# 32 tokens' experts by gathered rows, beside dense U and V for the other 224

## The reference

```python
q = (ht @ w_q).reshape(T, PEER_HEADS, 2, PEER_HALF)
scores = jnp.einsum('thcd,hckd->thck', q, sub_keys)
# top 16 of each half, top 16 of their sums -> idx, g = softmax(top_s)
act = jax.nn.gelu(jnp.einsum('pd,phkd->phk', hb, u[ib]))
out = jnp.einsum('phk,phkd->pd', gb * act, v[ib])
```

## Time and profile before

| | |
|---|---|
| device time, three runs | 2462.65 us median (2459.61 to 2463.94) |
| the profiled execution | span 2461.2 us from first to last instruction; its device time is not recorded apart |
| busy | PE 2372.8, DVE 1667.5, ACT 1447.1, POOL 498.6 us |
| granted TensorE clock | 0.992 over the span |
| DMA | 449.67 MB, 183 GB/s mean |

### The profile page before, as it was taken

How to read it: one execution, slowest core, us unless ns; L and a number is a source line. 1 busy time by engine, 2 the same in 40 slices (tenths; PEclk the granted TensorE clock), 3 DMA queues, 4 the chain that set the end, 5 groups by cost and what they waited for, 6 DMA issues and landing times.

```text
span 2461.2 us, 50127 instructions
## 1 busy us (share of the span) xinstructions
PE 2372.8 (96%) x16310; PEld 2175.1 (88%) x16314; DVE 1667.5 (68%) x3882; ACT 1447.1 (59%) x3296; POOL 498.6 (20%) x417
## 2 busy tenths in 40 slices
PE   8998989999999999999999989899999999999998
PEld 8997888999999878888899978889999998788887
DVE  5667775577876676666656667755778767666666
ACT  5576755555655655555555676555555556555555
POOL 0000200007767400000000003000177773000000
PEclk9999999999999999999999999999999999999999
DMA  5554465456666446566544535654566664466664
GB/s 207 191 186 142 167 246 177 152 180 187 172 188 172 137 145 222 216 210 220 198 148 171 175 134 203 213 179 154 179 184 176 187 182 109 171 221 213 219 216 162
DMA packets 165203, 449.67 MB, mean 183 GB/s; under 512 B 48060, under 2 KB 58228, under 8 KB 164852
## 3 DMA queue, kind: packets, MB, share of 16 engines
...
HBM read 429.44 MB, written 21.66 MB: 183 GB/s over the span
## 4 chain that ended last, share of the span: by engine, by line
PE 87%; ACT 5%; DVE 5%; issue 2%; DMA 2%; ACTq 0%; POOL 0%; DVEq 0%; POOLq 0%; SPq 0%
PE bank L301 16%; PE bank L303 16%; PE bank L302 16%; PE bank L316 10%; PE bank L318 10%; PE bank L317 10%; PE bank L1613 2%; DVE w_lo L283 2%; ACT w_hi L270 2%; DMA raw<-stream 1%; ACT L343 1%; PE bank L393 1%; PE bank L1073 1%; PE bank L1595 1%; PE bank L1046 1%
## 5 line engine op out<-in xcount | busy, mean ns | idle before, releaser
L283 DVE TENSOR_TENSOR w_lo<-raw,w_hi 128x512 fp32r<-128x512 f32 x1512 | 1027.6, 690 | 718.2 <-ACT w_hi L270 704.6
L270 ACT ACTIVATE w_hi<-raw 128x512 fp32r<-128x512 f32 x1512 | 904.5, 626 | 384.7 <-PE bank L318 313.0
L301 PE MATMUL bank<-h_hi,w_hi 128*128 128x256 f32 x3360 | 963.6, 287 | 14.1 <-DVE w_lo L283 13.9
L302 PE MATMUL bank<-h_lo,w_hi 128*128 128x256 f32 x3360 | 952.5, 283 | 0.0
L303 PE MATMUL bank<-h_hi,w_lo 128*128 128x256 f32 x3360 | 952.4, 283 | 0.0
L301 PEld LDWEIGHTS bank<-h_hi,w_hi 128*128 128x128 f32 x3360 | 646.2, 192 | 25.9 <-DVE w_lo L283 18.8
L302 PEld LDWEIGHTS bank<-h_lo,w_hi 128*128 128x128 f32 x3360 | 646.8, 193 | 0.5
L303 PEld LDWEIGHTS bank<-h_hi,w_lo 128*128 128x128 f32 x3360 | 646.5, 192 | 0.0
L1204 POOL DMA_INDIRECT spread_w<-mass,cell_at x256 | 429.1, 1676 | 444.7 <-DVE mass L1491 298.0
L316 PE MATMUL bank<-w_hi,a_hi 128*128 128x512 f32 x1088 | 426.9, 392 | 10.6 <-DVE a_lo L411 5.6
L317 PE MATMUL bank<-w_lo,a_hi 128*128 128x512 f32 x1088 | 426.0, 392 | 0.0
...
## 6 DMA issues: line engine op xcount, KB each, us to landing
...
spread_w<-zeros POOLq DMA_DIRECT2D x32, 512.0 KB, 15.2
h_hi<-spread_w POOLq DMA_DIRECT2D x32, 512.0 KB, 4.8
...
spread_w<-mass,cell_at POOLq DMA_INDIRECT x256
...
```

The costliest lines, as they stand in the source:

```text
L270: act.activation(w_hi[:, (ring % 2) * 2 + k, :], raw[:, slot, sub, 512 * k:512 * k + 512], ACT.Copy).then_inc(w_hi_done, 1)
L283: dve.tensor_tensor(w_lo[:, q, :], raw[:, slot, sub, 512 * k:512 * k + 512], w_hi[:, q, :].bitcast(F32), ALU.subtract).then_inc(w_parts, 1)
L301: pe.matmul(ps, hi, rhs_hi(4 * k + c), start=first, stop=False)
L302: pe.matmul(ps, hi, rhs_lo(4 * k + c), start=False, stop=False)
```

## The change

32 tokens of the first tile (its lanes 96 to 127) leave the dense path. h, `A` and the U matmuls keep 224 columns: first the second tile, then 96 tokens of the first. For the 32 tokens, ScalarE's queue copies their pick numbers (`own_at`) and weights (`mass`) to `lane`, where 128 lanes are 4 groups of 32 tokens with 32 picks each. 64 indirect gathers per layer on GpSimd's queue bring one row of 4 KB per lane into a ring of four (`row`): 32 of U, 32 of V. VectorE forms the 32 dots with `h_rep`, ScalarE their gelu, VectorE sums the weighted V rows in `own`. Two matmuls fold the four groups and VectorE adds the result to x. `h_rep` comes from two matmuls after the scores and a gain row loaded by SP. Rows 0 to 3 are fetched inside the scatters of head 6, rows 4 to 7 behind the last scatter, rows 8 to 63 between the fetches of `spread_w`. Dots 0 to 7 stand at eight of the last U blocks, dots 8 to 31 at every second V block from 0, the sums at every second V block from 48. Scatters and spread products cover 96 lanes. `spread_w` is 96 wide and is zeroed in pieces of 128 floats, six per partition, in place of two of 512. In V the first tile's stationary has 96 columns, the moving side stays 512.

```diff
+N_OWN = 32
+N_DENSE = SEQ - N_OWN
+N_FIRST = P - N_OWN
+LANE_GROUPS = P // N_OWN
+OWN_PICKS = P // LANE_GROUPS
+RING = 4
+EARLY_DOTS = 8
...
-        spread_w = [nc.dram_tensor(f"spread_w{l}", (P, KEYS, P), F32, kind="Internal").ap() for l in range(DEPTH)]
+        spread_w = [nc.dram_tensor(f"spread_w{l}", (P, KEYS, N_FIRST), F32, kind="Internal").ap() for l in range(DEPTH)]
...
+        MIX_COLS = (slice(0, P), slice(P, 2 * P))
+        PEER_COLS = (slice(P, P + N_FIRST), slice(0, P))
...
-                    pool.dma_start(spread_w[layer][8 * i:8 * i + 8].rearrange("e (a b) t -> (e a) (b t)", a=16).rearrange("p (n f) -> p n f", f=512),
-                                   spread(zeros[:].rearrange("p (n f) -> p n f", n=1), 1, 2)).then_inc(cleared.sem, 16)
+                    pool.dma_start(spread_w[layer][8 * i:8 * i + 8].rearrange("e (a b) t -> (e a) (b t)", a=16).rearrange("p (n f) -> p n f", f=128),
+                                   spread(zeros[:].rearrange("p (n f) -> p n f", n=1), 1, 6)).then_inc(cleared.sem, 16)
...
-            A = sb(part, "A", [P, KEYS, SEQ])
+            A = sb(part, "A", [P, KEYS, N_DENSE])
+            row = sb(part, "row", [P, RING, D])
+            h_rep = sb(part, "h_rep", [P, D])
+            lane = sb(part, "lane", [P, 2, OWN_PICKS])
+            lane_at = sb(part, "lane_at", [P, 2, OWN_PICKS], U32)
+            dots = sb(part, "dots", [P, OWN_PICKS])
...
+            DOT_AT = (-12, -11, -10, -9, -3, -2, -1, 0)
...
-            spread_tile = [h_hi[:, 4 * i:4 * i + 4, :].rearrange("p c s -> p (c s)").bitcast(F32).rearrange("p (k t) -> p k t", t=P) for i in range(2)]
+            spread_tile = [h_hi[:, 4 * i:4 * i + 3, :].rearrange("p c s -> p (c s)").bitcast(F32).rearrange("p (k t) -> p k t", t=N_FIRST) for i in range(2)]
...
+                def fetch_row(n):
+                    i, values = n % RING, n // OWN_PICKS
+                    if n >= RING:
+                        pool.wait_ge(row_used.sem, row_used.base + n - RING + 1)
+                    pool.indirect_dma_start(row[:, i, :], None, stream_rows if values else u_rows,
+                                            bass.IndirectOffsetOnAxis(ap=lane_at[:, values, n % OWN_PICKS:n % OWN_PICKS + 1], axis=0)).then_inc(row_in[i].sem, 16)
                 pool.wait_ge(cleared.sem, cleared.base)
...
-                        pool.indirect_dma_start(cells, bass.IndirectOffsetOnAxis(ap=cell_at[:, h, r:r + 1], axis=0), mass[:, h, r:r + 1], None,
+                        pool.indirect_dma_start(cells, bass.IndirectOffsetOnAxis(ap=cell_at[0:N_FIRST, h, r:r + 1], axis=0), mass[0:N_FIRST, h, r:r + 1], None,
                                                 compute_op=ALU.add).then_inc(scattered.sem, 16)
+                        if (h, r) == (6, 12):
+                            pool.wait_ge(lanes_done.sem, lanes_done.base + 1)
+                            pool.wait_ge(rep_done.sem, rep_done.base + 1)
+                            for n in range(RING):
+                                fetch_row(n)
+                for n in range(RING, 2 * RING):
+                    fetch_row(n)
                 pool.wait_ge(scattered.sem, scattered.base + 16 * P)
                 pool.wait_ge(up_read.sem, up_read.base + 2 + B_V)
                     pool.dma_start(spread_tile[i % 2], spread_w[layer][:, 8 * i:8 * i + 8, :]).then_inc(spread_in[i % 2].sem, 16)
                 fetch(0)
                 fetch(1)
-                for i in range(2, 16):
-                    pool.wait_ge(spread_done.sem, spread_done.base + i - 1)
-                    fetch(i)
+                for n in range(2 * RING, 2 * OWN_PICKS):
+                    if n % 4 == 0 and n // 4 < 16:
+                        i = n // 4
+                        pool.wait_ge(spread_done.sem, spread_done.base + i - 1)
+                        fetch(i)
+                    fetch_row(n)
...
+                sp.dma_start(row[:, 0, :], spread(ffn_g[layer:layer + 1], 0, P)).then_inc(gain_row_in.sem, 16)
...
+                        if r == 2 and k == at + 6:
+                            act.wait_ge(own_kept.sem, own_kept.base + 2)
+                            act.wait_ge(mass_done.sem, mass_done.base + 2)
+                            for g in range(LANE_GROUPS):
+                                for i, kept in enumerate((own_at, mass)):
+                                    act.dma_start(lane[N_OWN * g:N_OWN * g + N_OWN, i, :].rearrange("p (h k) -> p h k", h=PEER_HEADS), kept[N_FIRST:P, :, 4 * g:4 * g + 4]).then_inc(lanes_in.sem, 16)
...
+                eights(0, 6)
+                act.wait_ge(row_used.sem, row_used.base + OWN_PICKS)
+                act.activation(dots[:], dots[:], ACT.Gelu_apprx_tanh).then_inc(own_gelu.sem, 1)
+                eights(6, 15)
...
+                def repeat_own():
+                    dve.wait_ge(rep_mm.sem, rep_mm.base + 1)
+                    dve.wait_ge(gain_row_in.sem, gain_row_in.base + 16)
+                    for k in range(2):
+                        cols = slice(512 * k, 512 * k + 512)
+                        ins = dve.tensor_tensor(h_rep[:, cols], row[:, 0, cols], bank[4 + k][:, :], ALU.mult)
+                    ins.then_inc(rep_done.sem, 1)
+                def lane_rows():
+                    dve.wait_ge(lanes_in.sem, lanes_in.base + 2 * LANE_GROUPS * 16)
+                    code = lane[:, 0, :]
+                    num, key = whole[:, 0:OWN_PICKS], dots[:]
+                    ch(dve.tensor_copy(num, code))
+                    dve.tensor_scalar(lane_at[:, 0, :], code, float(layer * KEYS * KEYS), None, ALU.add)
+                    ch(dve.tensor_scalar(num, num, 7, None, ALU.logical_shift_right))
+                    ch(dve.tensor_copy(key, num))
+                    ch(dve.tensor_scalar(code, code, float(KEYS), float(first_row_v(layer)), ALU.mult, ALU.add))
+                    dve.scalar_tensor_tensor(out=lane_at[:, 1, :], in0=key, scalar=float(1 - KEYS * KEYS), in1=code, op0=ALU.mult, op1=ALU.add).then_inc(lanes_done.sem, 1)
                 def masses(r):
...
+                        dve.tensor_copy(own_at[N_FIRST:P, mine, :], sel_i[N_FIRST:P, 0:ROUND_HEADS[r], :]).then_inc(own_kept.sem, 1)
+                        dve.tensor_scalar(cell_at[:, mine, :], sel_i[:, 0:ROUND_HEADS[r], :], float(N_FIRST), consts[:, C_ROW:C_ROW + 1], ALU.mult, ALU.add)
                         half(2)
...
+                def row_dot(i, wait, to):
+                    dve.wait_ge(row_in[i].sem, wait)
+                    dve.scalar_tensor_tensor(out=row[:, i, :], in0=row[:, i, :], scalar=1.0, in1=h_rep[:], op0=ALU.mult, op1=ALU.mult, accum_out=to).then_inc(row_used.sem, 1)
...
+                    n = DOT_AT.index(b - B_V) if b - B_V in DOT_AT else None
+                    if n is not None:
+                        row_dot(n % RING, row_in[n % RING].base + 16 * (n // RING + 1), dots[:, n:n + 1])
...
+                spread_product(0, 0, 0, 0)
+                part_lo(dve, src, 0, 0, N_DENSE)
+                dve.memset(own, 0.0)
+                ch(dve.tensor_scalar(turn_own, iota, consts[:, C_LANE:C_LANE + 1], None, ALU.is_equal))
+                def sixteen(n, first, i):
+                    if i in (3, 11):
+                        spread_product(1 - i // 8, n, first, 1 + i // 8)
+                    k = 16 * first + i
+                    split_lo(dve, n * 16 + (B_V + k + 1), (i + 1) % 4)
+                    part_lo(dve, src, n * 16 + (k + 1), (i + 1) % 2, N_DENSE)
+                with dve.Fori(0, 3) as n:
                     for i in range(16):
-                        if i in (3, 11):
-                            spread_product(1 - i // 8, n, 1 + i // 8)
-                        ahead_v(n * 16 + i, n * 16 + (B_V + i), i % 4, n, i)
+                        sixteen(n, 0, i)
+                        if i % 2 == 0:
+                            j = EARLY_DOTS + i // 2
+                            row_dot(j % RING, n * 32 + (row_in[j % RING].base + 16 * (j // RING + 1)), dots[:, bass.ds(n * 8 + j, 1)])
+                dve.wait_ge(own_gelu.sem, own_gelu.base + 1)
+                ch(dve.tensor_tensor(dots[:], dots[:], lane[:, 1, :], ALU.mult))
+                with dve.Fori(0, 4) as n:
+                    for i in range(16):
+                        sixteen(n, 3, i)
+                        if i % 2 == 0:
+                            j = i // 2
+                            dve.wait_ge(row_in[j % RING].sem, n * 32 + (row_in[j % RING].base + 16 * ((OWN_PICKS + j) // RING + 1)))
+                            dve.wait_ge(row_used.sem, n * 8 + (row_used.base + OWN_PICKS + j))
+                            dve.scalar_tensor_tensor(out=own, in0=row[:, j % RING, :], scalar=dots[:, bass.ds(n * 8 + j, 1)], in1=own, op0=ALU.mult, op1=ALU.add).then_inc(row_used.sem, 1)
                 for k in range(112, N_V - 1):
                     if k == 115:
-                        spread_product(1, 7, 1)
-                    ahead_v(k, B_V + k, k % 4, None, None)
```

(55 more changed lines are left out.)

115 lines of the change are left out of this document (63 added, 52 removed).

## The result

The changed kernel takes 2507.44 us (median of 4 runs, 2502.28 to 2512.37), the kernel before on the same chip 2461.13 (4 runs, 2457.65 to 2463.94). Ratio 1.0188, 95% interval 1.0171 to 1.0205. The profiled execution has a span of 2500.5 us, against 2461.2.

A forecast was written before the change was run, and what follows sets the result against it. TensorE was taken as the bound (87% of the chain). Per layer U -17.8, V +5.8 and zero writes +2 us gave -10, -20 in all: span 2441, median 2442.5 us; own range 2428 to 2456, whole range 2410 to 2528.

The forecast's parts named there:

- The failed step: V, per layer: +5.8 us, bounds 1.8 and 20, with DMA engines at 80 to 85% and VectorE fitting its blocks.
- 2498 (4): Rival, V: VectorE becomes the bound if a dot or sum takes over 1.9 us; at 2.4 us, 2498; chance 0.10.
- rival 1: GpSimd in U: scatters get no cheaper with 96 lanes, row 4 is 46 us late, 2527 us; chance 0.20.
- U's columns: TensorE in U: 224 columns bring matmul spacing from 120 to 112 ns, a gain of 24.6 us per layer.
- The lane copies: ScalarE in U block 62: eight copies, some 4 us, mostly covered by idle time and buffer, cost 1 us.
- The scatters: GpSimd beside U: 96 lanes, not 128, at 10.3 ns per lane make each scatter 0.33 us shorter.
- the wait for row 4: End of U: row 4 lands at 805.5 us, needed at 801.5, so 4 us late per layer.
- V's pace: TensorE in V: moving side sets the 226 ns matmul spacing, so the 96-column stationary gains nothing.
- VectorE in V: V: a dot or sum takes 1.27 us, bringing VectorE to 2.40 of 2.71 us per block: it fits.
- Zero writes: Mixing: each of 16 writes takes 1.46 us, not 0.727; 2 us per layer, bounds 0 and 16.

The follow-up runs named there:

- e2: Changed kernel, with V's 24 dots and 32 sums on 16 of 1024 elements, gathers whole: 2505.7 us, ratio 1.0207.
- e10: Kernel before, with only its U matmuls cut from 256 to 224 columns of h, nothing replacing the 32 tokens: 2416.3 us, ratio 0.9822.
- e5: e4 plus lane copies one per block, rows 4 to 7 fetched between the last scatters, zero writes behind the power: 2472.4 us, ratio 1.0057.
- e4: Changed kernel, with each spread_w fetch two gathers later on GpSimd's queue: 2477.2 us, ratio 1.0071.
- e9: e5 with rows 0 to 7 fetched inside heads 5 and 6, dots 0 to 7 moved, V's first stationary 128 columns wide: 2454.6 us, ratio 0.9975.
- e11: e9 with the eight early gathers one by one between scatters and zero writes at the head of GpSimd's expert part: 2455.1 us, ratio 0.9974.

## Why the prediction was wrong

The failed step is V's: it was to grow by 5.8 us per layer and grew by 20.5 and 25.9. Two terms in U were mis-sized beside it. The measured 2507 lies between the rivals' 2498 (4) and 2527 (1), but by the way of neither: VectorE was not V's bound (e2), and U, which rival 1 made longer, became shorter.

- **U's columns: right.** 112 ns taken, 112 in a plain block and 113 on the mean measured; e10 gives 22.2 us per layer against 24.6.
- **The lane copies: mis-sized.** The idle time and the two-block buffer were to "cover most: 1 us"; it was 6.2 us (blocks 62 and 63; gone in e5). ScalarE's idle 45% lies between blocks in pieces of up to about 1.5 us, and eight issues in a row (5.4 us) don't fit into one.
- **The scatters: mis-sized.** 10.3 ns per lane was worked out from a plain transfer; 128 to 96 lanes gave 0.144 us, 96 to 64 nothing. That lies below the 0.25 us at which rival 1 put the turn. It alone did not make the kernel slow, because the ends that the prediction held against each other both moved: the wait for row 4 was 6.5 us, against 4.
- **V: the step that failed.** The prediction put the DMA engines at 80 to 85% ("below full, 0, up to 5 us if bursts meet"). The mean was no higher (0.76). The bursts meet once in 8 blocks, and each makes ScalarE wait up to 4.8 us, because GpSimd's queue holds gathers behind a fetch that waits for a spread product and lets all go at once. Only two slots of `raw` stand between the stream and ScalarE. The diff shows that order; the prediction named the queue and did not follow what waits in it. e4 prices it: 11.0 and 15.4 us of V. What is left in e4 over the kernel before, 9.5 and 10.5 us, is the pace below and stalls of 3.9 and 3.5.
- **V's pace: not seen.** "TensorE gains nothing" was taken to mean that it loses nothing. Each matmul lost 4 ns to the 96-column stationary, by spacing 6 us per layer; e9 got back 2.5 per layer. Why such a stationary slows the pace is open. Some 5 us more of the second V came from the low clock behind TensorE's pauses; no term of the sum had that.
- **VectorE in V: right.** 1.22 and 1.28 us per dot and sum for 1.27; e2 shows that they were not the bound.
- **Zero writes: 2 us was 5.3 and 1.7.** Not the time of a write: there is a pause of 13 us once ten are out, and moving the writes did not bring mixing back (e5, e11). That their traffic is the reason was not shown, since no run left them out. Fewer, larger pieces were not tried.
